# A two-block transformer kernel: projections of latents and values moved into the second mixer's first rounds, its last output products into the last two, and scores issued ahead of older transposes

## What is computed

```python
z = rms_norm_2(h, mix_pre_g[l]) @ w_in[l]                 # 1024 -> 3*512 + 256 + 128 + 32
q_na, k_na, v_na, c_q, c_kv, k_rope = jnp.split(z, split_at, axis=-1)
o_na = neighbourhood_attention(q_na, k_na, v_na, na_rpb[l])      # 8 heads, windows of 8 x 16
o_mla = latent_attention(c_q, c_kv, k_rope, q_norm_g, w_uq, kv_norm_g, w_ukv, cos, sin)
mixed = jnp.concatenate([rms_norm_2(o_na, na_out_norm_g[l]),
                         rms_norm_2(o_mla, mla_out_norm_g[l])], axis=-1) @ w_out[l]
h = h + rms_norm_2(mixed, mix_post_g[l])
```

## Time and profile before

| | us |
|---|---|
| median of 3 runs (1889.76 to 1890.82) | 1890.28 |
| the profiled execution | 1895.27 |
| its span, first to last instruction | 1893.5 |
| TensorE busy | 1799.1 (95%) |
| VectorE, ScalarE, POOL busy | 962.5, 858.8, 255.7 |
| mean granted TensorE clock (1.00 is full) | 0.973 |
| share of the chain that ended last: TensorE, VectorE, ScalarE | 88%, 6%, 2% |
| SyncE's issue of the 16 DMAs into `Vband` (L934) | 10.40 |

### The profile page before, as it was taken

The page is one execution under the profiler, slowest core; times in us unless marked ns, Lnnn a source line. Parts: engine busy times, 40 slices in busy tenths (PEclk is TensorE's granted clock), DMA queues, the critical chain, the costliest instruction groups (busy, mean ns, idle before and its releaser), DMA issues.

```text
span 1893.5 us, 22854 instructions
## 1 busy us (share of the span) xinstructions
PE 1799.1 (95%) x8643; PEld 1427.0 (75%) x8643; DVE 962.5 (51%) x1545; ACT 858.8 (45%) x1346; POOL 255.7 (14%) x315
## 2 busy tenths in 40 slices
PE   8998999999869999998999999998899999999998
PEld 6886666666758888867888888776577678888886
DVE  4546344435368999975342334453655454323434
ACT  4236565552338888863231323242566442223222
POOL 4001532220001111120000000070223100000000
PEclk9998999998979999999999999999899999999999
DMA  7224011113469999674423332243101223324331
GB/s 213 89 70 134 23 45 45 45 45 127 184 250 348 378 391 385 258 237 141 111 89 98 92 105 95 78 124 108 48 16 46 67 78 89 111 78 111 89 111 56
DMA packets 161316, 246.59 MB, mean 130 GB/s; under 512 B 11362, under 2 KB 117057, under 8 KB 148288
## 3 DMA queue, kind: packets, MB, share of 16 engines
q1 hardware_dynamic: 152912, 232.57, 36.5%
q0 software_dynamic: 8304, 12.69, 2.2%
HBM read 239.42 MB, written 12.61 MB: 133 GB/s over the span
## 4 chain that ended last, share of the span: by engine, by line
PE 88%; DVE 6%; ACT 2%; issue 2%; DMA 1%; POOL 0%; SPq 0%; DVEq 0%; ACTq 0%
PE psum L473 25%; PE psum L475 24%; PE psum L474 24%; PE psum L625 3%; PE psum L653 3%; PE psum L609 3%; PE psum L1355 1%; ACT warea_r L433 1%; PE psum L631 1%; DVE warea_r L439 1%; DVE xarea L2522 1%; DVE arena L2128 0%; DVE harea L2110 0%; DVE xarea L2123 0%; DMA xarea<-in_x 0%
## 5 line engine op out<-in xcount | busy, mean ns | idle before, releaser
L439 DVE TENSOR_TENSOR warea_r<-warea,warea_r 128x2048 fp32r<-128x2048 f32 x108 | 250.7, 2322 | 315.0 <-ACT warea_r L433 314.8
L473 PE MATMUL psum<-tarea_r,warea_r 128*128 128x512 f32 x916 | 365.7, 399 | 4.2 <-DVE tarea_r L2161 3.2
L474 PE MATMUL psum<-tarea_r,warea_r 128*128 128x512 f32 x916 | 358.7, 392 | 0.0
L475 PE MATMUL psum<-tarea_r,warea_r 128*128 128x512 f32 x916 | 358.6, 392 | 0.0
L473 PE MATMUL psum<-warea_r,arena_r 128*128 128x512 f32 (+1 forms) x768 | 300.9, 392 | 11.7 <-DVE warea_r L410 3.5
L433 ACT ACTIVATE warea_r<-warea 128x2048 fp32r<-128x2048 f32 x108 | 205.9, 1907 | 221.6 <-PE psum L475 219.1
L475 PE MATMUL psum<-warea_r,arena_r 128*128 128x512 f32 (+1 forms) x768 | 298.1, 388 | 0.0
L474 PE MATMUL psum<-warea_r,arena_r 128*128 128x512 f32 (+1 forms) x768 | 297.8, 388 | 0.0
L473 PEld LDWEIGHTS psum<-tarea_r,warea_r 128*128 128x128 f32 x916 | 173.0, 189 | 48.4 <-issue 10.2
L475 PEld LDWEIGHTS psum<-tarea_r,warea_r 128*128 128x128 f32 x916 | 173.1, 189 | 36.9
L474 PEld LDWEIGHTS psum<-tarea_r,warea_r 128*128 128x128 f32 x916 | 173.2, 189 | 34.5 <-issue 0.7
(11 more groups left out here) (337 smaller groups left out, 2413.8 us busy)
## 6 DMA issues: line engine op xcount, KB each, us to landing
warea<-in_ffn_w_gu SPq DMA_DIRECT2D x88, 512.0 KB, 5.0
warea<-in_w_in SPq DMA_DIRECT2D x40, 512.0 KB, 4.6
warea<-in_ffn_w_down SPq DMA_DIRECT2D x40, 512.0 KB, 4.1
arena<-in_w_up SPq DMA_DIRECT2D x16, 1024.0 KB, 7.7
tarea<-in_w_up SPq DMA_DIRECT2D x16, 1024.0 KB, 7.4
tarea<-in_w_down SPq DMA_DIRECT2D x16, 1024.0 KB, 7.5
warea<-in_w_gate SPq DMA_DIRECT2D x14, 1024.0 KB, 7.8
harea<-in_w_gate SPq DMA_DIRECT2D x14, 1024.0 KB, 8.3
```

The lines of the kernel that those rows point to most:

```text
L439: dve.tensor_tensor(w_lo[:, u % 2, :], raw_of(u), w_hi[:, u % 2, :].bitcast(f32), ALU.subtract)\
L473: nc.tensor.matmul(out, high, by_high, start=first, stop=False)
L474: nc.tensor.matmul(out, high, by_low, start=False, stop=False)
L475: return nc.tensor.matmul(out, low, by_high, start=False, stop=last)
```

## The change

Latents are projected ahead of values. K's two units are followed at once by round 0, and the two projections are fill: latent tiles r in rounds 0 to 3 (two half tiles a round, banks 6, 4, 5, 7), values in rounds 4 to 7 (two half results a round). Tables 0 to 2 are made between K's two halves, 3 in round 0, 4 and 5 in round 4, 6 and 7 in round 8. The latents are transposed in rounds 8 and 9, the latent jobs run from round 11 to 18, value products of units 0 and 1 stand in rounds 10 and 11 (so their transposed blocks need room of their own, `j0`). The 16 DMAs into `Vband` start in two halves after V's evacuation in rounds 7 and 8. Norm sums move from round 20 to 19, output jobs to rounds 21, 22, 24, 25, 27, 28, 30, 31. In the tail, 9 of the last 36 output products are fill of round 32 and 18 of round 33; 9 stay behind the last value product. In both mixers, a round's scores are issued ahead of the transposes of round d-2. The diff, cut to its core:

```diff
     ffn("ffn1", 0)
-    for n, (lo, hi) in enumerate(((0, 512), (512, 1024), (1024, 1536))):
+    for n, (lo, hi) in enumerate(((0, 512), (512, 1024), (1536, 1952), (1024, 1536))):
         for h in range(2):
             unit([(0, hi - lo, chunks(w_in2, 4 * h, 4 * h + 4, lo, hi))], *(("z2_psum", 4 * n + 4) if h else ()))
-    for h in range(2):
-        unit([(0, 416, chunks(w_in2, 4 * h, 4 * h + 4, 1536, 1952))], "z2_psum", 16)
...
+TABLE_ROUND = {1: (3,), 5: (4, 5), 9: (6, 7)}
+TABLE_BANK = (0, 1, 2, 7, 7, 5, 4, 5)
+LATENT_BANK, VALUE_BANK = (6, 4, 5, 7), (6, 5, 4, 7)
+JOBS_AT, PV_LATE = 11, {10: (0,), 11: (1,)}
+OUT_BANK = ((6, 0, 1, 2), (3, 4, 5, 6))
 MLA_JOBS = ([("qn", 0), ("qr", 0), ("kn", 0)] + [("v", t) for t in range(NT)]
             + [(kind, p) for p in range(1, 4) for kind in ("qn", "qr", "kn")])
 BY_ACT = ("qn", "kn")
-OUT_ROUND = {d: i for i, d in enumerate((22, 23, 24, 26, 27, 28, 30, 31))}
+OUT_ROUND = {d: i for i, d in enumerate((21, 22, 24, 25, 27, 28, 30, 31))}
 ENDS = {x[0]: m for m, items in enumerate(FILL) for x in items}
 
 
...
+        if ph["name"] == "second" and d <= max(PV_LATE):
+            return PV_LATE.get(d, ())
         st = ph["steps"][2 * (d - LAG)] if 0 <= d - LAG < len(ph["steps"]) // 2 else None
-        return st["u"] if st and st["last"] else None
+        return (st["u"],) if st and st["last"] else ()
 
...
-                if 0 <= m:
-                    st = steps[m]
-                    if n0 + m >= 2:
-                        pe.wait_ge(s["pt_ready"], n0 + m - 1)
-                    pe.wait_ge(*scaled(n0 + m))
-                    bank, pbuf = ps[2 + st["e"]], st["pb"][:, (n0 + m) % 4, :]
-                    for j, (c0, rows) in enumerate(st["blocks"]):
-                        mm = nc.tensor.transpose(bank[0:rows, P * j:P * j + P], pbuf[:, c0:c0 + rows], ident)
-                    mm.then_inc(s["pt_psum"], 1)
             if d < rounds:
                 two = steps[2 * d:2 * d + 2]
                 if n0 + 2 * d >= 2:
...
-            u = unit_ends(ph, d)
-            if u is not None:
+            for m in range(2 * (d - LAG), 2 * (d - LAG) + 2):
+                if 0 <= m:
+                    st = steps[m]
+                    if n0 + m >= 2:
+                        pe.wait_ge(s["pt_ready"], n0 + m - 1)
+                    pe.wait_ge(*scaled(n0 + m))
+                    bank, pbuf = ps[2 + st["e"]], st["pb"][:, (n0 + m) % 4, :]
+                    for j, (c0, rows) in enumerate(st["blocks"]):
+                        mm = nc.tensor.transpose(bank[0:rows, P * j:P * j + P], pbuf[:, c0:c0 + rows], ident)
+                    mm.then_inc(s["pt_psum"], 1)
+            if fill and d < rounds:
+                fill(d)
+            elif fill and ph["name"] == "second":
+                fill(d)
+            for u in unit_ends(ph, d):
                 unit = units[u]
                 pair = ph["p0"] + unit["pair"]
-                pe.wait_ge(s["pt_ready"], n0 + 2 * (d - LAG) + 2)
+                pe.wait_ge(s["pt_ready"], n0 + 2 * NT * (u + 1))
...
                     nj, rows = len(st["blocks"]), st["rows"]
                     src = ps[2 + st["e"]][0:rows, 0:P * nj].rearrange("p (j q) -> p j q", j=nj)
...
-                    sp.wait_ge(s["z2_evac"], 4)
-                    for b, band in enumerate((0, 8, 24, 32)):
-                        for r in range(4):
+                    for r in range(4):
+                        if r % 2 == 0:
+                            sp.wait_ge(s["z2_evac"], 6 + r)
+                        for b, band in enumerate((0, 8, 24, 32)):
...
                     for r in range(4):
                         q = 4 * n + r
-                        if q >= 8 and h == 0:
...
-                    if n == 2 and h == 0:
+                    if n == 1 and h == 0:
                         pe.wait_ge(s["xrev_in"], 16 * 8 * H)
-                        pe.wait_ge(s["z2_first"], 8)
-                        for g in range(2):
-                            na_table(g, ps[6 + g])
...
+                        pe.wait_ge(s["z2_first"], 3)
+                        for g in range(3):
+                            na_table(g)
+            pe.wait_ge(s["na_tab"], 3)
+            pe.wait_ge(s["z2_first"], 5)
+
+            def latent(r, h):
+
+                u = AT_MID + 4 + h
...
+                if h == 0:
+                    pe.wait_ge(*((s["z2_first"], (7, 5, 6)[r]) if r < 3 else (s["na_tab"], 4)))
...
+                    pe.wait_ge(*((s["z2_evac"], (1, 3, 2)[r]) if r == 0 or r == 2 else (s["na_tab"], 6)))
...
+                if d == 4:
+                    pe.wait_ge(s["z2_evac"], 4)
+                    for g in (4, 5):
+                        na_table(g)
+                if d < 4:
+                    for r in range(2 * (d % 2), 2 * (d % 2) + 2):
+                        latent(r, d // 2)
+                elif d < 8:
+                    for r in (d % 2, d % 2 + 2):
+                        values(r, (d - 4) // 2)
+                if d == 0:
+                    pe.wait_ge(s["z2_first"], 8)
+                    na_table(3)
+                if d == 8:
+                    pe.wait_ge(s["z2_evac"], 8)
+                    for g in (6, 7):
+                        na_table(g)
+                if d in (8, 9):
+                    latent_turned(2 * (d - 8))
+                    latent_turned(2 * (d - 8) + 1)
+                if d in PV_LATE:
+                    pe.wait_ge(s["na_tab"], H)
...
-                if d == 20:
...
-
-            attend_pe(pe, second, na_table, second_fill)
-
-            pe.wait_ge(s["pt_ready"], second["n0"] + len(second["steps"]))
-            pe.wait_ge(s["split_lo"], AT_MID + 12 + 1)
-            for t in range(NT):
-                out_product(ps[t], 1, 0, t, range(3))
-            pe.wait_ge(s["o_evac"], 16)
+                if d == 2 * MLA_AT:
+                    pe.wait_ge(s["split_lo"], AT_MID + 12 + 1)
+                    pe.wait_ge(s["o2_first"], 7)
+                    pe.wait_ge(s["o_evac"], 15)
+                    out_product(ps[OUT_BANK[0][0]], 1, 0, 0, range(3))
+                if d == 2 * MLA_AT + 1:
+                    pe.wait_ge(s["scored"], second["n0"] + len(second["steps"]))
+                    for t in (1, 2):
+                        out_product(ps[OUT_BANK[0][t]], 1, 0, t, range(3))
+
+            attend_pe(pe, second, fill=second_fill)
+
+            out_product(ps[OUT_BANK[0][3]], 1, 0, 3, range(3))
             pe.wait_ge(s["o2_first"], 8)
             norm_sums(1)
...
-            for n in range(3):
+            for n in range(2):
                 split_high(AT_MID + 2 * n + 2)
                 if n == 0:
                     row_copy(3, ps[7])
-                for r in range(4 if n > 1 else 0):
-                    q = 4 * n + r
-                    act.wait_ge(s["z2_psum"], q + 1)
-                    nc.scalar.activation(v2[:, r, :], ps[q % 8], ACT.Identity, scale=late[3][:, r:r + 1]).then_inc(s["z2_evac"], 1)
...
+                for r in {3: (0, 1), 4: (2, 3)}.get(d, ()):
+                    act.wait_ge(s["z2_psum"], 8 + r + 1)
+                    nc.scalar.activation(z3[:, r, :], ps[LATENT_BANK[r]][:, 0:416], ACT.Identity, scale=late[3][:, r:r + 1])\
                         .then_inc(s["z2_evac"], 1)
...
+                if d in (2, 4):
+                    split_high(AT_MID + 5 + d // 2)
                 if d == 5:
+                    root(rstd[:, 16:24])
```

More of the change, by code:

```diff
@@ L501, in make_phase @@
                         st = dict(u=u, g=2 * pair + e_, e=e_, first=i == 0, last=i == NT - 1, mask=False, gate=None,
[L502 removed]
+                                  table=None, shift=0, scale=-1.0, rows=P, dst=P * i, rot=None, j0=2 * (pair % 2) if kind == "na" else 0,
                                   pb={"fox": PB, "nsa": PB, "na": PB2, "mla": PBm}[kind])
@@ L574, in tables_at @@
     def tables_at(ph, d):
+        if ph["name"] == "second":
+            yield from TABLE_ROUND.get(d, ())
+            return
         for g, group in enumerate(ph["groups"]):
@@ L697, in attend_dve @@
                     recip(m - 1)
-            u = unit_ends(ph, d)
-            if u is not None and ph["units"][u]["last_of_pair"]:
-                evac(u)
+            for u in unit_ends(ph, d):
+                if ph["units"][u]["last_of_pair"]:
+                    evac(u)
             if fill:
@@ new lines, in values @@
+            def values(r, h):
+                u = AT_MID + 6 + h
+                if r == 0:
+                    pe.wait_ge(s["split_lo"], u + 1)
+                if h == 0:
+                    pe.wait_ge(*((s["z2_evac"], (1, 3, 2)[r]) if r == 0 or r == 2 else (s["na_tab"], 6)))
+                for c in range(4):
+                    k = 4 * h + c
+                    mm = products(ps[VALUE_BANK[r]], hT_hi[:, k, P * r:P * r + P], hT_lo[:, k, P * r:P * r + P],
+                                  *weights(u, 512 * c, 512), k == 0, k == KD - 1)
+                if h:
```

(3 more changed lines are left out.)

164 lines of the change are left out of this document (71 added, 93 removed).

## The result

| | before | after |
|---|---|---|
| median, us | 1890.55 (1889.76 to 1892.33, 4 runs) | 1866.87 (1865.11 to 1867.19, 4 runs) |
| the profiled execution | 1895.27 | 1867.19 |
| its span | 1893.5 | 1865.4 |
| TensorE busy | 1799.1 | 1781.5 |

The ratio is 0.9864, 95% interval 0.9847 to 0.9882: faster by **23.7 us** in the medians, where 11.2 were forecast, and just under the range. The profiled executions differ by 28.1, since that of before stands 5.0 over its median and that of after 0.3. TensorE has the same 8643 matmuls and is busy 17.6 us less with them: the first sign that the gain is not waits alone. The granted clock explains a part: 0.973 of 1893.5 us before and 0.977 of 1865.4 after leave 51.1 and 42.9 us missing, 8.2 less.

What follows compares the result with a forecast made beforehand. The prediction took TensorE, busy 95% of the span, as the bound, so only its waits and slow clock could be won. Terms of -17.1, +2.5 and +3.4 gave -11.2 us, from 1890.3 to 1879, range 1867 to 1886.

Steps and rivals of the forecast that it cites:

- (7): First mixer: new order leaves the distance from scores to scores unchanged; taken as 0, bounds 4 us off to 5 on.
- (1) to (3): Second mixer, K's end to round 15: 24.0 us not work before, 6.9 of waits left, so 17.1 us off.
- V's band: Second mixer, near unit 0's value product: transfers might delay it by 1 to 2 us, left in the range.
- (4): Second mixer's last rounds: scores first adds waits, 4.8 us before scores 21, 24 and 27; net 2.5 us on.
- (5): Second mixer's end: 27 output products moved into rounds 32 and 33 take the same TensorE time there; nothing won.
- (6): Clock: two falls at 1.7 us each, counted for the waits the new order leaves; 3.4 us on.
- not work: K's end to scores of round 15, before the change: 17.2 us of TensorE waits plus 6.8 of slow clock, 24.0.
- Rival A: Second mixer: remaining waits hidden, clock full; 27 us off, 1863, or "half of it, 1870"; chance 0.16.
- Rival C: First mixer's 62 rounds: reduces wait for older transposes, up to 0.5 us each; 31 us slower, 1910; chance 0.04.

Runs made afterwards that it cites:

- b_share: The kernel before, order and waits unchanged, with VectorE instead of POOL scaling every second step of the first mixer: 1890.61 us, ratio 0.9994.
- b_warm: The kernel before with ten small products between the two steps' transposes in rounds 30, 42 and 54 of the first mixer: 1890.05 us, ratio 1.0000.
- a_warm: The changed kernel with ten small products ahead of the scores of rounds 30, 42 and 54 of the first mixer: 1862.73 us, ratio to before 0.9842.
- b_sf1: The kernel before with scores issued ahead of the older transposes in the first mixer only: 1883.69 us, ratio 0.9957.
- a_again: The changed kernel unaltered, measured again beside other runs: 1866.82 us, ratio to the kernel before 0.9867.

## Why the prediction was wrong

**The step that failed is (7), "Its rounds get the same new order ... I take 0".** The first mixer's order gained 4.7, 6.4 and 8.3 us in three comparisons of medians, against bounds of 4 off to 5 on. Two things were missed. First, POOL's scales came late in the early rounds: 3.0 us of gaps, half of them in no view, so "its whole idle time is 6.5 us" was no upper bound for a gain. With scores first the transposes come 1.3 us later behind the fill (204.09 to 205.43 above), and POOL is through. Rounds 2 to 17 went from 66.8 to 62.4, of which `b_share` gives 2.9 to the gaps. Second, the step said that the distance from scores to scores "stays fill plus one round's transposes", as if an instruction's price did not depend on its neighbours. It does. Mean distances from start to start, worked out from the traces of the two runs at full clock in rounds 18 to 62 (`b_warm`, `a_warm`):

| last of / first of | old order, us | new order, us |
|---|---|---|
| fill, then transposes / scores | 0.232 (33) | 0.366 (33, some short waits in it; median 0.327) |
| value product, then transposes / scores | 0.289 (11, some short waits in it; median 0.203) | 0.203 (7) |
| transposes, then scores / fill | 0.206 (43) | 0.028 (44) |
| scores, then fill / transposes | 0.246 (44) | 0.247 (44) |

The three steps of a round add up to 0.68 and 0.64 us behind fill, and to 0.74 and 0.48 behind a value product; with the two medians in place of the means, 0.68 and 0.60, 0.66 and 0.48. The Trainium skill (TensorEngine Tiling (Array Packing), Tiling Modes) lets TensorE drain wherever the tiling changes, here in front of the scores, whose weights have 64 rows, and behind them. Both orders have as many such changes, so by it alone they would cost the same; the sums of this table don't agree. That the price depends on the neighbour is thus measured; why is not shown. A round without any wait is 0.08 us shorter (3.52 and 3.44 from scores to scores, before and after), and at full clock the 44 rounds 3.0:

```profile
334.03 0.41 PE L625 MATMUL psum<-small,arena 64*128 64x31 f32 x4
337.55 0.49 PE L625 MATMUL psum<-arena 64*128 64x128 f32 x4
```
```profile
325.74 0.41 PE L624 MATMUL psum<-small,arena 64*128 64x31 f32 x4
329.18 0.49 PE L624 MATMUL psum<-arena 64*128 64x128 f32 x4
```

The part of (7) on the long wait was right: 4.7 us in three waits for POOL, the 1.74 of the earlier trace rows among them, became 5.1 in four for the reduce.

So the 10.9 us that the two profiles differ by in the first mixer are 0.3 ahead of its round 2, 4.4 in rounds 2 to 17 and 6.1 behind them. Of the 6.1, 3.0 are the order's own and 3.1 are luck: 13.6 us at half clock in the one execution, 6.8 in the other. With the small products in the long waits (`b_warm`, `a_warm`) the whole of it differs by 8.0 (248.3 and 240.3).

**(1) to (3), right in kind, small by 1.6.** Forecast 6.9 us of waits from K's end to round 15, measured 5.3 of idle time, of which 1.8 for latent job 6's bank (forecast 2.1), 0.9 and 0.3 for jobs 2 and 3 (1.2 and 0.5), 1.1 before scores (2.1 in all). V's band was late by 0.4. No wait of rounds 0 to 7 is among them.

**(4), mechanism right, net too high by 2.5.** Waits of 5.0 where 4.8 were forecast, and 0.7 for 0.8. The late rounds lost 0.5, not the 3.4 that the step has for them (4.8 + 0.8 - 0.87 - 1.31), and the end won 0.5, not 0.9. The idle time in the late rounds did rise by 3.5 (5.7 for 2.2), but nine products of latent jobs (132 before, 123 after; 9 x 0.23 = 2.1) had moved ahead of round 15 with the jobs' start, one round earlier, and four transposes (116 for 120, some 0.5) out behind round 31, which the step did not count. The nine products stand in the 84.4 of the front.

**(5), too low as a part.** The products cost the same there as here, but without them the new order would have made the end 2.2 longer than before (408.2 for 406.0): they cover a wait for the copies of 2.1, where (4) had 0.9.

**(6), one fall for two.** 3.5 us at 0.51 near 1354: 1.7 us by length times missing share, as the step reckons; in the first mixer a us at half clock cost less than that half (0.32 to 0.41, above). No fall followed the three waits of 1.67 in the late rounds, while a wait of 1.69 in the first mixer had one behind it (3.5 us at 0.52 from 292), and so had one of 1.43 (3.4 at 0.50 from 336.5). The Trainium skill (TensorE: Matmul & The Clock Gate, HAM oscillation — how this bites in real kernels) lets the clock fall only behind idle gaps longer than any of these waits. The falls behind 1.43 and 1.69 and the one in `b_sf1` without any wait speak against it; the late rounds fit it. Of 24.0 us that counted as "not work", 6.8 were clock of one execution which itself stood 5.0 over its median.

The sum again, in the profiles: forecast 13.7 off for (1) to (3) and (6) and 2.5 on for (4) and (5); measured 17.4 off and nothing (0.5 lost in the late rounds, 0.5 won behind them). The rest of the miss is the first mixer, 10.9, less 0.2 elsewhere. The front's 17.4 are its waits and clock (24.0 before, 5.3 and 1.7 after), for its work is nearly the same: nine products came (2.1), three tables went into K's projection (six matmuls, 1.6 from 1259.75) and four transposes behind the scores of round 15 (0.5). Rival A gave the right time (1863 to 1872) for another reason: the waits of (3) and (4) were not hidden. Its "half of it, 1870" is about half of the way from the forecast to 1863; half of its 27 us would have been 1877. Rival C asked the right question, the room of the first mixer's rounds, and had its sign wrong. The reduces do wait for the transposes now (VectorE 71.3 us in 41 times, where it had waited 85.9 for scores), but that cost TensorE little, and its transposes stopped waiting for POOL in the early rounds.

## What to carry to other kernels

Before costing a reorder at nothing, measure the distance from start to start across each kind of neighbour and the gap inside each group of like instructions: here a wait of 0.24 us on TensorE counted as busy and showed in no list of waits. Idle time is then no upper bound for what an order can give. Where a profiled execution stands some us over its median, leave its clock falls out of the sum, and fill the rounds without work before moving work out of those that have it.

## What the runs showed of the hardware

- A matmul's modelled end hides the first 0.17 us of a wait behind transposes: 0.59 us lost, 0.42 shown.
- What an instruction costs depends on its neighbour: an fp32r product starts 0.03 us after the last transpose, scores with 64-row weights 0.21 after it (table above).
- The same wait, of 1.2 to 1.7 us in the view, is followed by half clock in some executions and not in others, at 0.32 to 0.41 us lost for each us of it; and half clock comes with no wait before it (`b_sf1`, 1405.3). Ahead of their first difference too: `a_again` has half clock from 161.4 to 164.7 and from 178.5 to 181.8, `a_warm`, the same code up to 280, in the second of the two alone.
- Filling three such waits with ten small products each brought 4.1 us in one order and nothing in the other. This is not explained.
